# A decoder layer with 32 experts on one core: the two transposes of a unit side by side, two projection tiles in lockstep, and a table for the experts' order

## The chip, the cores and the metric
One core of one Trainium2 chip runs the whole layer in one launch, in float32. The metric is the device time in microseconds (us), median over runs.

## The reference
One inference step of a layer, for 1024 prompt tokens and 8 single-token samples, width 1024:
```python
u = layer_norm(x) * (1.0 + scale) + shift            # shift, scale, gates: m = silu(c) @ w_ada + b_ada
proj = u @ w_in                                      # 1024 -> 4624 columns
x_l, g_l, z, xbc, dt_raw = split(proj)
y_l = rms_norm(rglru(causal_conv(x_l)) * gelu(g_l))  # Griffin RG-LRU heads
y_s = rms_norm(ssd(silu(causal_conv(xbc)), dt) * silu(z))   # Mamba-2 heads
x = layer_norm(alpha * x + gate * (concat(y_l, y_s) @ w_out))
v = layer_norm(x) * (1.0 + scale2) + shift2
# top-1 group of 4, then top-2 of its 8 experts for each token
for each token t and each of its 2 experts e:
    f[t] += gate_weight * (silu(v[t] @ w_gate[e]) * (v[t] @ w_up[e])) @ w_down[e]     # 1024 -> 512 -> 1024
x = layer_norm(alpha * x + gate2 * f)
```
The counts of tokens by expert come out of the router at run time; any counts are allowed.

## The kernel before
Each engine has one program, and they meet by semaphores. The order of all work is written by hand; there is no scheduler. Products that need float32 accuracy are made from high and low halves (a slice of the left side times a slice of the right in the three combinations of PARTS).

**Front.** SP loads x tiles, pairs of columns of w_ada (`load_pair`) and the projection weights of a tile (`load_w`, 512 KB). VectorE normalises the eight tiles of x (L1132 to L1141), PE transposes each (`x_turn`, L885), GpSimd issues the small loads, b_ada in two layouts among them (badaP for the first two rows of modulation, bada4 for the others). Then the modulation: PE multiplies one of four pairs (`ada_pair`, L895), VectorE adds the bias (L1176), PE turns the result (L902), and VectorE scales two of the eight slices k of u by it and splits each into high and low (`u_pair`, `u_low` L1192). The projection of a tile of 128 columns (`project_split`, L939) is 72 matmuls: eight slices k, three PARTS, three pieces of 344 tokens. Its weights are split by ScalarE (`w_high`) and VectorE (`w_low`). Tile 0 goes slice by slice as u becomes ready, with pairs 2 and 3 of the modulation in it; tile 1 follows. Behind each of the first eight tiles stands a late pair (L877), which computes the remaining modulation rows. A tile's result is copied out before its PSUM bank is used again (`px_copied`).

**The experts.** 32 places in an order that the table rank_at gives: the first three places are experts 0 to 2, and the others get the remaining experts by rank of their number of units, rank 3 the largest; GpSimd writes the table with two iotas and copies, big ranks at every third place, small ones between. A unit is up to 32 tokens of one expert, a token being four rows of 256. For unit u:

- GpSimd gathers its rows of v into xg (L1851) by an index column that VectorE copies (icur, L2589), and stores its result by scur (L1859, L2593).
- PE turns the rows (`x_turn`, L2207), VectorE copies them to xT (`x_out`, L2577).
- PE multiplies with gate and up in four chunks q (`gate_up`, L2219, x64 in the trace, two records for each float32 matmul). ScalarE copies h out (`hb_out`, L1990) and makes its half of the activation (L1995).
- PE turns h (`h_turn`, L2228), VectorE forms the product (`h_out`, L2581, L2585), PE multiplies with down (`down`, L2237, x32), and ScalarE copies the result out (L2000).

PE's order is h_turn(u), gate_up(u+1), x_turn(u+2), down(u). VectorE's order is h_out(u), up_copy(u+2), gather_rows(u+4) and the rest. When unit u+2 starts a new expert, `up_copy` copies its up weights from the ring to wcur in four chunks (L2619), each after the matmuls that read that part of wcur, with x_out of the unit between the second and the third. ScalarE does the same with the gate weights (L2020), with hb_out between the second and the third. `down_copy` (L2632) moves the down weights behind the last down of the expert before.

SP loads all experts' weights into a ring with three slots for gate/up (4 MB) and two for down (2 MB). Its loop is serial, x from 2:
```python
sp.wait_ge(down_copied, copied_down(x - 1)); load_down(x + 1, e)
down_here(x)
gate_up_here(x + 1)
if 5 <= x + 2 < NE - 1:
    gate_up_when_copied(x + 2, x - 1)
if x + 3 == NE - 1:
    gate_up_when_copied(x + 3, x)
```
`gate_up_here` waits for the landing and tells ScalarE and VectorE; `gate_up_when_copied` waits until both have copied the weights that the slot held.

Of the kernel before, what the change touches and what calls it, by code (L numbers as in the profile page):

```python
# [25 lines left out]
ALU = mybir.AluOpType  # L26
# [54 lines left out]
def build_step(nc, x_prompt, x_sample, c_prompt, c_sample, state_lru_conv, state_lru_h, state_ssd_conv,  # L81
# [13 lines left out]
    with ctx:  # L95
# [113 lines left out]
        modP, badaP = at(46300, 4, P), at(43904, 4, P)  # L209
# [65 lines left out]
        bada_loaded = sem("bada_loaded")  # L275
        pair_loaded = [sem(f"pair_loaded{c}") for c in range(4)]
# [110 lines left out]
        with nc.Block() as block:  # L387
            @block.sync
            def _(sp):
# [113 lines left out]
            def _(gp):  # L503
# [8 lines left out]
                for g in range(4):  # L512
                    gp.dma_start(bada4[32 * g:32 * g + 32, :, :],
                                 b_ada.rearrange("a (r g n) -> g a r n", r=3, g=4)[g].to_broadcast([32, 3, 512]))\
                        .then_inc(bada_loaded, 16)
                for g in range(4):
                    gp.dma_start(badaP[32 * g:32 * g + 32, :, :],
                                 b_ada[:, 0:2 * D].rearrange("a (s c i n) -> s i a c n", s=2, c=4, i=2)[g // 2, g % 2]
                                 .to_broadcast([32, 4, P])).then_inc(bada_loaded, 16)
# [33 lines left out]
                gp.tensor_copy(qidx[:, :], itmp[:, :]).then_inc(gpsimd_once, 1)  # L553
                gp.wait_ge(xnT_mm, NT)
                for b in range(2):
                    gp.memset(xb2[b][:, 0:3], 0.0).then_inc(gpsimd_once, 1)

# [100 lines left out]
            def _(act):  # L658
# [57 lines left out]
                for k in range(KT):  # L716
                    if k == 5:
                        w_high(1, 0)
# [146 lines left out]
            def _(pe):  # L865
# [23 lines left out]
                def ada_pair(c):  # L889
                    pe.wait_ge(pair_loaded[c], 32)  # L890
                    if c > 1:
                        pe.wait_ge(mod0_ready, c - 1)
                    for k in range(KT):
# [27 lines left out]
                ada_pair(0)  # L921
                ada_pair(1)
# [3 lines left out]
                def project_split(b, w_round, by_slice=False, half_way=None):  # L926
                    pe.wait_ge(wh_ready[b], w_round + 1)
                    pe.wait_ge(wl_ready[b], w_round + 1)
                    for k in range(KT):
                        if half_way is not None and k == KT // 2:  # L930
                            half_way()
                        if by_slice and k in (2, 4):
                            ada_pair(k // 2 + 1)
# [1817 lines left out]
```

## Time and profile before
| what | value |
|---|---|
| median of 3 runs | 1520.05 us (1520.03 to 1522.19) |
| profiled execution | 1519.19 us |
| its span | 1517.4 us |
| mean granted clock of TensorE | 0.951 |
| PE busy | 1361.2 us, 90% |
| VectorE (DVE) busy | 969.7 us, 64% |
| ScalarE (ACT) busy | 574.1 us, 38% |
| GpSimd (POOL) busy | 296.7 us, 20% |
| mean DMA rate | 241 GB/s over the span |
| experts' stage | first gate_up at 913.29, last down ends at 1451.13 |

Times in a row are from the start of the span, and durations are in us. A row of a timeline gives in brackets how long the engine had been idle and what released it; "issue" means that it waited for nothing that the trace shows. PEld is the weight load, which overlaps PE. Matmul ends are modelled, so a run of matmuls in a row is read best from start to start.

### The profile page before, as it was taken

What the parts mean: (1) busy time and instruction counts of PE and PEld (TensorE: products, weight loads), DVE (VectorE), ACT (ScalarE), POOL (GpSimd) and SP (SyncE); (2) the same over time, 40 slices, a digit from 0 to 9 for tenths busy, and PEclk for the clock granted to TensorE, in tenths of its full rate; (3) what the DMA queues carried; (4) which work ended last, traced back from release to release, by engine and by line L of the source; (5) the groups of instructions that cost most, each with busy time, mean ns of one, the idle gap of its engine ahead of it and who ended that gap; (6) DMA issues with size and microseconds to landing.
All of it is one profiled execution on the core that took longest, in us unless ns stands there. A gap on an engine that the chain in (4) does not pass through costs nothing.

```text
span 1517.4 us, 38240 instructions
## 1 busy us (share of the span) xinstructions
PE 1361.2 (90%) x13487; PEld 1007.3 (66%) x13487; DVE 969.7 (64%) x1720; ACT 574.1 (38%) x886; POOL 296.7 (20%) x325
## 2 busy tenths in 40 slices
PE   4799999999999999799999539999999899999964
PEld 3688989899888889578588525554455455555421
DVE  6755553958999998888687674544454353351649
ACT  4322232535655555732132104433343243241532
POOL 4000002211000000200000013443333343443310
PEclk9899999999999999899999759999999999999987
DMA  9666414644333434932332948999999988979683
GB/s 279 220 228 247 144 42 157 210 154 143 114 113 114 123 117 155 337 105 70 99 90 81 367 187 321 416 409 415 413 409 398 404 356 367 400 283 416 265 322 153
DMA packets 145042, 365.87 MB, mean 241 GB/s; under 512 B 16072, under 2 KB 94976, under 8 KB 117192
## 3 DMA queue, kind: packets, MB, share of 16 engines
q1 hardware_dynamic: 126072, 308.72, 54.6%
q0 software_dynamic: 18320, 54.08, 10.0%
q10 hardware_dynamic: 576, 2.10, 0.4%
q8 instruction: 45, 0.74, 0.2%
q14 instruction: 29, 0.24, 0.0%
HBM read 324.06 MB, written 45.63 MB: 244 GB/s over the span
## 4 chain that ended last, share of the span: by engine, by line
PE 31%; DMA 16%; DVE 7%; issue 2%; SPq 1%; ACT 1%; ACTq 0%; DVEq 0%; POOLq 0%
DMA ring<-in_w_up_dram 14%; PE PS L2088 10%; PE PS L2219 10%; PE PS L2237 5%; DMA ring<-in_w_down_dram 2%; PE PS L2228 1%; DVE big L2289 1%; PE PS L2119 1%; PE PS L2207 1%; PE PS L2154 1%; DVE ring L2687 1%; DVE ring L2692 1%; PE PS L2111 1%; DVE ring L2701 1%; DVE big_end L2301 1%
## 5 line engine op out<-in xcount | busy, mean ns | idle before, releaser
L939 PE MATMUL PS<-big 128*128 128x344 f32 x2592 | 425.2, 324 | 1.7 <-DVE big L1192 1.7
L939 PEld LDWEIGHTS PS<-big 128*128 128x128 f32 x2592 | 414.2, 190 | 10.5 <-issue 6.7
L2219 PE MATMUL PS<-ring,arena 128*32 128x256 f32 x5248 | 306.4, 386 | 0.5 <-DVE arena L2577 0.5
L2219 PEld LDWEIGHTS PS<-ring,arena 128*32 128x32 f32 x5248 | 164.3, 111 | 113.5 <-issue 6.5
L2020 ACT ACTIVATE ring<-ring 128x1024 f32 x124 | 124.0, 1049 | 94.1 <-PE PS L2219 52.4
L2237 PE MATMUL PS<-ring,arena 128*32 128x256 f32 x2624 | 158.6, 382 | 1.0 <-DVE arena L2585 1.0
L1851 POOL DMA_INDIRECT arena<-v_d,icur x84 | 103.0, 1226 | 283.1 <-DVE icur L2589 191.3
L1859 POOL DMA_INDIRECT f_d<-arena,scur x82 | 107.7, 1313 | 55.3 <-issue 48.6
L2237 PEld LDWEIGHTS PS<-ring,arena 128*32 128x32 f32 x2624 | 77.0, 109 | 57.1 <-issue 13.4
L2581 DVE SCALAR_TENSOR_TENSOR arena<-arena,PS 128x128 f32<-128x128 f32 x82 | 23.6, 288 | 135.4 <-ACT arena L1995 97.5
L2577 DVE COPY arena<-PS 128x256 f32<-128x256 f32 x82 | 34.7, 423 | 103.9 <-PE PS L2207 103.8
L2619 DVE COPY ring<-ring 128x1024 f32 x124 | 80.6, 692 | 25.7 <-SPq L1712 20.0
L1990 ACT ACTIVATE arena<-PS 128x256 f32<-128x256 f32 x82 | 31.4, 382 | 170.2 <-PE PS L2219 170.2
L2088 PE MATMUL PS<-low 128*128 128x512 f32 x256 | 83.7, 409 | 10.5 <-issue 4.9
L2632 DVE COPY ring<-ring 128x4096 f32 x31 | 74.7, 2409 | 28.6 <-PE PS L2237 28.6
L2088 PE MATMUL PS<-big,low 128*128 128x512 f32 x256 | 81.3, 400 | 0.0
L2088 PE MATMUL PS<-low,big 128*128 128x512 f32 x256 | 81.0, 398 | 0.0
L2000 ACT ACTIVATE arena<-PS 128x256 f32<-128x256 f32 x82 | 31.4, 383 | 100.5 <-PE PS L2237 96.4
L2088 PEld LDWEIGHTS PS<-low 128*128 128x128 f32 x256 | 47.4, 194 | 21.7 <-issue 8.1
L1154 DVE TENSOR_TENSOR big<-arena,big 128x1024 fp32r<-128x1024 f32 x20 | 24.5, 1224 | 56.6 <-ACT big L713 56.5
L2228 PEld LDWEIGHTS PS<-ident,arena 128*128 128x128 f32 x164 | 26.0, 207 | 50.7 <-issue 29.6
L2228 PE MATMUL PS<-ident,arena 128*128 128x128 f32 x164 | 41.9, 338 | 16.9 <-ACT arena L1990 16.7
(473 smaller groups left out, 1876.5 us busy)
## 6 DMA issues: line engine op xcount, KB each, us to landing
ring<-in_w_gate_dram SPq DMA_DIRECT2D x32, 2048.0 KB, 9.6
ring<-in_w_up_dram SPq DMA_DIRECT2D x32, 2048.0 KB, 14.9
ring<-in_w_down_dram SPq DMA_DIRECT2D x32, 2048.0 KB, 8.1
arena<-in_w_ada_dram SPq DMA_DIRECT2D x16, 1024.0 KB, 6.7
arena<-in_w_in_dram SPq DMA_DIRECT2D x20, 512.0 KB, 7.8
upper<-in_w_ada_dram SPq DMA_DIRECT2D x8, 1024.0 KB, 11.6
upper<-in_w_in_dram SPq DMA_DIRECT2D x16, 512.0 KB, 4.0
arena<-acs_d SPq DMA_DIRECT2D x8, 1024.0 KB, 4.9
```

What stands on the lines that cost most here:

```text
L939: mm = pe.matmul(PS[:, 3 * b + a, 0:CU], wss[b][:, i, k, :], us[:, j, k, a * CU:(a + 1) * CU], start=(k == 0 and (i, j) == PARTS[0]), stop ...
L1851: gp.indirect_dma_start(xg[b], None, v_q, bass.IndirectOffsetOnAxis(ap=icur[b][:, :], axis=0), bounds_check=QW * (SEQ + DEC) - 1, oob_is_e ...
L1859: gp.indirect_dma_start(f_q, bass.IndirectOffsetOnAxis(ap=scur[b][:, :], axis=0), yo[b], None, bounds_check=QW * 2 * (SEQ + DEC) - 1, oob_ ...
L1990: act.activation(hb, PS[:, 3, 0:FH], ACT.Copy).then_inc(hb_ready, 1)
L2020: act.activation(wcur[:, 1024 * q:1024 * q + 1024], ring[:, bass.ds(w + 1024 * q, 1024)], ACT.Copy).then_inc(gate_copied, 1)
L2088: mm = pe.matmul(PS[:, bank + n, :], (yh[h % 2], yl3[h % 3])[a][:, k, :], (WH, WL)[b][i][:, 512 * n:512 * n + 512], start=(k == 0 and (a, ...
L2219: mm = pe.matmul(PS[32 * g:32 * g + 32, 3, 0:FH], xT[:, c, CAP * q:CAP * q + CAP], wcur[:, w:w + FH], start=(q == 0 and c == 0), stop=(q = ...
L2228: mm = pe.transpose(PS[:, 4, P * c:P * c + P], hb[:, c::2], ident[:, :])
L2237: mm = pe.matmul(PS[32 * g:32 * g + 32, 6, 0:DQ], hT[:, c % 2, CAP * (c // 2):CAP * (c // 2) + CAP], wcur[:, 8192 + 1024 * c + DQ * g:8192 ...
L2577: ve.tensor_copy(xT, PS[:, 0, 0:2 * P].rearrange("p (c t) -> p c t", c=2)).then_inc(xT_ready, 1)
L2619: ve.tensor_copy(wcur[:, 4096 + 1024 * q:5120 + 1024 * q], ring[:, bass.ds(w + (4096 + 1024 * q), 1024)]).then_inc(up_copied, 1)
L2632: ve.tensor_copy(wcur[:, GU:GU + DN], ring[:, bass.ds(w, DN)]).then_inc(down_copied, 1)
```

## The change
Three parts.

**Front.** SP posts the second tile's weights right behind the first's. The loads of badaP wait until PE has turned two tiles of x, those of bada4 until the last pair of w_ada has landed. The turn of a pair's modulation is a function of its own (`ss_turn`), and tiles 0 and 1 are computed slice by slice in turn: slice k of tile 0, then slice k of tile 1. VectorE makes the low half of the second tile's weights in front of slice 1 instead of slice 6, ScalarE its high half at k = 1 instead of 5. The late pairs stand one tile later, and the loop over the last four tiles is written out.

**Unit.** PE's order becomes h_turn(u), x_turn(u+2), gate_up(u+1), down(u); xT has two buffers; VectorE copies x and the index column at the start of its turn, ahead of h_out.

**Places.** The ranks come from a written table PLAN, one memset for each place from 3 on.

```diff
@@ SP
                 load_pair(0)
                 load_w(COL_XBC, 0)
+                load_w(COL_XBC + P, 1)
                 load_pair(1)
                 load_pair(2)
-                load_w(COL_XBC + P, 1)
                 load_pair(3)
@@ GpSimd, front (the two loops of loads stood ahead of the load of xt[NT])
+                gp.wait_ge(xnT_mm, 2)
+                for g in range(4):
+                    gp.dma_start(badaP[32 * g:32 * g + 32, :, :],
...
                 gp.wait_ge(xnT_mm, NT)
                 for b in range(2):
                     gp.memset(xb2[b][:, 0:3], 0.0).then_inc(gpsimd_once, 1)
+                gp.wait_ge(pair_loaded[3], 32)
+                for g in range(4):
+                    gp.dma_start(bada4[32 * g:32 * g + 32, :, :],
...
@@ ScalarE
                 for k in range(KT):
-                    if k == 5:
+                    if k == 1:
                         w_high(1, 0)
@@ PE, front
+                def ss_turn(c):
                     pe.wait_ge(mod0_ready, c + 1)
-                    if c > 1:
-                        pe.wait_ge(ss_ready, c - 1)
-                    pe.transpose(PS[:, 4 + c % 2, 0:P], modP[:, c, :], ident[:, :]).then_inc(ss_mm, 1)
+                    pe.transpose(PS[:, 6 + c % 2, P:2 * P], modP[:, c, :], ident[:, :]).then_inc(ss_mm, 1)
...
+                for k in range(KT):
+                    c = k // 2
+                    if k in (2, 4):
+                        ada_pair(c + 1)
+                    pe.wait_ge(uh_ready, k + 1)
+                    pe.wait_ge(ul_ready, k + 1)
+                    for b in range(2):
...
+                        mm = slice_products(b, k)
+                        if k == KT - 1:
+                            mm.then_inc(proj_mm[b], 1)
+                        if b == 0 and k % 2 == 0 and c < 3:
+                            ss_turn(c + 1)
...
+                late_pair(0)
+                for t in range(2, 12):
+                    pe.wait_ge(px_copied[t % 2], t // 2)
+                    project_split(t % 2, t // 2)
+                    if t < 9:
+                        late_pair(t - 1)
@@ VectorE, front
                 u_pair(0)
                 w_low(0, 0)
                 u_low(0)
+                u_pair(1)
+                w_low(1, 0)
                 u_low(1)
-                u_pair(1)
                 u_low(2)
                 u_low(3)
-                lam_rates()
                 u_pair(2)
                 u_low(4)
                 u_low(5)
                 u_pair(3)
-                w_low(1, 0)
...
+                lam_rates()
@@ experts, table
-        FIRST, EVERY = 3, 3
-        NBIG = (NE - FIRST) // EVERY
+        FIRST = 3
+        PLAN = [24, 23, 5, 16, 8, 7, 13, 3, 14, 26, 27, 6, 15, 4, 12, 28, 0, 11, 18, 22, 2, 19, 17, 9, 1, 25, 10, 20, 21]
...
+                step(gp.tensor_copy(rank_at[:, 0:FIRST], eidx[:, 0:FIRST]))
+                for x, r in enumerate(PLAN):
+                    step(gp.memset(rank_at[:, FIRST + x:FIRST + x + 1], float(FIRST + r)))
@@ experts, PE
                 with pe.Fori(1, pairs) as j:
                     for b in range(2):
                         h_turn(j * 2 + b)
-                        gate_up(j * 2 + (b + 1))
                         x_turn(j * 2 + (b + 2), j + 1, b)
+                        gate_up(j * 2 + (b + 1), 1 - b)
                         down(j * 2 + b)
@@ experts, VectorE
+                def x_out_next(u, b):
+                    ve.wait_ge(gu_mm, (u - 1) * QW)
+                    x_out(u, b)
...
                         for q in range(QW):
-                            if q == 2:
-                                x_out(u)
                             ve.wait_ge(gu_mm, before * QW + (q + 1))
...
                 with ve.Fori(1, pairs) as j:
                     for b in range(2):
+                        x_out_next(j * 2 + (b + 2), b)
+                        gather_rows(j * 2 + (b + 4), b)
                         h_out(j * 2 + b)
                         up_copy(j * 2 + (b + 2), j * 2 + (b + 1))
-                        gather_rows(j * 2 + (b + 4), b)
                         scatter_rows(j * 2 + b, j, b)
```

**The order on the engines.** First PE at the front, from the end of the transposes of x on. L895 (L899 after) is a pair of the modulation, L902 (L906) its turn, L939 (L934) the projection products, L877 (L880) a late pair. Before:
```order
L895 MATMUL PS<-upper 32x128 x32
L902 MATMUL PS<-ident,upper 128x128
L895 MATMUL PS<-upper 32x128 x32
L902 MATMUL PS<-ident,upper 128x128
L939 MATMUL PS<-big 128x344 x18
L895 MATMUL PS<-upper 32x128 x32
L902 MATMUL PS<-ident,upper 128x128
L939 MATMUL PS<-big 128x344 x18
```
and changed:
```order
L899 MATMUL PS<-upper 32x128 x32
L906 MATMUL PS<-ident,upper 128x128
L899 MATMUL PS<-upper 32x128 x32
L934 MATMUL PS<-big 128x344 x9
L906 MATMUL PS<-ident,upper 128x128
L934 MATMUL PS<-big 128x344 x27
L899 MATMUL PS<-upper 32x128 x32
L934 MATMUL PS<-big 128x344 x9
L906 MATMUL PS<-ident,upper 128x128
L934 MATMUL PS<-big 128x344 x27
```
Nine products now stand between a pair and its turn, and the products between two pairs are 36 instead of 18.

Second, PE in the experts' loop, one pair of units. L2228 (L2245) is the turn of h, L2219 (L2236) gate_up, L2207 (L2224) the turn of x, L2237 (L2254) down. Before:
```order
L2228 MATMUL PS<-ident,arena 128x128 x2
L2219 MATMUL PS<-ring,arena 32x256 x32
L2207 MATMUL PS<-ident,arena 128x128 x2
L2237 MATMUL PS<-ring,arena 32x256 x16
L2228 MATMUL PS<-ident,arena 128x128 x2
L2219 MATMUL PS<-ring,arena 32x256 x32
L2207 MATMUL PS<-ident,arena 128x128 x2
L2237 MATMUL PS<-ring,arena 32x256 x16
```
and changed:
```order
L2245 MATMUL PS<-ident,arena 128x128 x2
L2224 MATMUL PS<-ident,arena 128x128 x2
L2236 MATMUL PS<-ring,arena 32x256 x32
L2254 MATMUL PS<-ring,arena 32x256 x16
L2245 MATMUL PS<-ident,arena 128x128 x2
L2224 MATMUL PS<-ident,arena 128x128 x2
L2236 MATMUL PS<-ring,arena 32x256 x32
L2254 MATMUL PS<-ring,arena 32x256 x16
```
The turn of x moved from behind gate_up to ahead of it.

Third, VectorE in the experts' loop after the change, the head of a unit: L2593 copies x out, L2609 the index column of a gather, L2601 and L2605 form the product of h, L2637 copies up weights.
```order
L2593 COPY arena<-PS 128x256
L2609 COPY icur<-arena 128x1
L2601 SCALAR_TENSOR_TENSOR arena<-arena,PS 128x128
L2605 SCALAR_TENSOR_TENSOR arena<-arena,PS 128x128
L2631 COMPARE_AND_BRANCH
L2632 ISA
L2637 ISA
L2637 COPY ring<-ring 128x1024
```
Before, the copy of x (L2577) stood in the middle of the four weight copies (L2619), behind the product of h (L2581, L2585), and the index column after them.

## Rows read from the trace of the kernel before
**Rows 1.** Page, part 2: busy tenths of POOL and of the DMA engines, 40 slices
```profile
POOL 4000002211000000200000013443333343443310
...
DMA  9666414644333434932332948999999988979683
```

**Rows 2.** Chain of waits, 1318 to 1332: start us, us, what
```profile
1318.66 3.59 PE PS L2219 x64
1322.25 0.37 PE PS L2207 x2
1322.61 1.86 PE PS L2237 x32
1324.48 0.44 PE PS L2228 x2
```

**Rows 3.** Page, part 5: groups of the experts' gate_up and turn of h
```profile
L2219 PE MATMUL PS<-ring,arena 128*32 128x256 f32 x5248 | 306.4, 386 | 0.5 <-DVE arena L2577 0.5
...
L2228 PE MATMUL PS<-ident,arena 128*128 128x128 f32 x164 | 41.9, 338 | 16.9 <-ACT arena L1990 16.7
```

**Rows 4.** PE's timeline, 1415 to 1452: start us, us, engine, line [idle before <-releaser]
```profile
1433.99 0.50 PE L2228 MATMUL PS<-ident,arena 128*128 128x128 f32 x2 [3.09 <-ACT arena L1990]
1434.42 5.35 PE L2219 MATMUL PS<-ring,arena 128*32 128x256 f32 x64
...
1442.37 3.66 PE L2219 MATMUL PS<-ring,arena 128*32 128x256 f32 x64
1445.84 1.91 PE L2237 MATMUL PS<-ring,arena 128*32 128x256 f32 x32
```

**Rows 5.** VectorE's timeline at the front, 0 to 90
```profile
10.89 1.29 DVE L1132 BATCH_NORM_STATS2 lnst<-arena 128x6 f32<-128x512 f32 x2 [1.87 <-DMA arena<-in_x_prompt_dram]
...
16.10 1.29 DVE L1132 BATCH_NORM_STATS2 lnst<-arena 128x6 f32<-128x512 f32 x2 [0.94 <-DMA arena<-in_x_prompt_dram]
...
45.00 2.37 DVE L1192 TENSOR_TENSOR big<-arena,big 128x1032 fp32r<-128x1032 f32 x2
```

**Rows 6.** PE's timeline at the front, 0 to 100
```profile
27.82 1.09 PE L885 MATMUL PS<-ident,arena 128*128 128x128 f32 x8 [1.22 <-DVE arena L1141]
...
47.84 4.61 PE L939 MATMUL PS<-big 128*128 128x344 f32 x18
...
67.59 3.05 PE L939 MATMUL PS<-big 128*128 128x344 f32 x18 [1.70 <-DVE big L1192]
...
72.42 11.63 PE L939 MATMUL PS<-big 128*128 128x344 f32 x72
```

**Rows 7.** Timeline of all engines before place 18, 1176 to 1194
```profile
1184.92 0.70 PE L2228 MATMUL PS<-ident,arena 128*128 128x128 f32 x2 [6.41 <-ACT arena L1990]
...
1186.92 0.28 ACT L1995 ACTIVATE arena<-PS 128x128 f32<-128x128 f32 x1
...
1188.31 0.29 DVE L2585 SCALAR_TENSOR_TENSOR arena<-arena,PS 128x128 f32<-128x128 f32 x1
```

**Rows 8.** Timeline of all engines at the start of the experts' stage, 900 to 945
```profile
909.04 1.14 POOL L1851 DMA_INDIRECT arena<-v_d,icur  x1 [4.70 <-issue]
...
912.39 0.38 PE L2207 MATMUL PS<-ident,arena 128*128 128x128 f32 x2
...
914.14 1.00 POOL L1851 DMA_INDIRECT arena<-v_d,icur  x1 [2.63 <-DVE icur L2589]
...
921.48 0.20 PEld L2207 LDWEIGHTS PS<-ident,arena 128*128 128x128 f32 x2 [0.41 <-DMA arena<-v_d,icur]
```

**Rows 9.** The same timeline, last down of place 1; chain of waits, whole span (last three)
```profile
940.63 1.93 PE L2237 MATMUL PS<-ring,arena 128*32 128x256 f32 x32
...
948.24 16.53 DMA ring<-in_w_up_dram
966.73 14.71 DMA ring<-in_w_up_dram
...
1166.81 15.55 DMA ring<-in_w_up_dram
```

More of the change, by code:

```diff
@@ L511, in _ @@
                 gp.memset(cT, 0.0).then_inc(c_zeroed, 1)
[L512 to L519, printed above, removed]
                 gp.dma_start(xt[NT], x_sample[:, 0, :]).then_inc(xt_loaded[NT], 16)
@@ L921, in _, with slice_products, project_split @@
                 ada_pair(0)
+                ss_turn(0)
                 ada_pair(1)
                 PARTS = ((0, 0), (0, 1), (1, 0))
-                def project_split(b, w_round, by_slice=False, half_way=None):
+                def slice_products(b, k):
+                    for i, j in PARTS:
+                        for a in range(3):
+                            mm = pe.matmul(PS[:, 3 * b + a, 0:CU], wss[b][:, i, k, :], us[:, j, k, a * CU:(a + 1) * CU],
+                                           start=(k == 0 and (i, j) == PARTS[0]),
+                                           stop=(k == KT - 1 and (i, j) == PARTS[-1]))
+                    return mm
+                def project_split(b, w_round, half_way=None):
                     pe.wait_ge(wh_ready[b], w_round + 1)
@@ L952, in _ @@
                         ada(6 + n // KT, n % KT, late[n % 2]).then_inc(late_mm, 1)
-                with pe.Fori(4, 6) as i:
-                    for b in range(2):
-                        pe.wait_ge(px_copied[b], i)
-                        project_split(b, i)
+                late_pair(0)
[4 more added lines that the diff above has]
+                        late_pair(t - 1)
                 pe.wait_ge(uh_ready, KT + 1)
@@ L1165, in _ @@
                 ve.tensor_tensor(lamv[0], lamv[2], PT1[:, :, 7], ALU.max).then_inc(vector_once, 1)
[L1167 removed]
+                ve.wait_ge(bada_loaded, 64)
                 step(ve.tensor_scalar(badaP[64:128, :, :], badaP[64:128, :, :], 1.0, None, ALU.add))
[L1169 removed]
                 ve.wait_ge(xnT_ready, NT)
@@ L1244, in mod_out @@
                 def mod_out(r):
+                    if r == 1:
+                        ve.wait_ge(bada4_loaded, 64)
+                        step(ve.tensor_scalar(bada4[0:64, 2, :], bada4[0:64, 2, :], 1.0, None, ALU.add))
                     ve.wait_ge(late_mm, KT * r)
@@ L2208, in x_turn, with gate_up @@
                     mm.then_inc(eT_mm, 1)
-                def gate_up(u):
+                def gate_up(u, b):
                     pe.wait_ge(xT_ready, u + 1)
@@ L2244, in _ @@
                 x_turn(0, 0, 0)
-                gate_up(0)
+                gate_up(0, 0)
                 x_turn(1, 0, 1)
@@ L2248, in _ @@
                     h_turn(u)
-                    gate_up(u + 1)
                     x_turn(u + 2, 1, u)
+                    gate_up(u + 1, 1 - u)
                     down(u)
@@ L2254, in _ @@
                         h_turn(j * 2 + b)
-                        gate_up(j * 2 + (b + 1))
                         x_turn(j * 2 + (b + 2), j + 1, b)
+                        gate_up(j * 2 + (b + 1), 1 - b)
                         down(j * 2 + b)
                 h_turn(pairs * 2)
-                gate_up(pairs * 2 + 1)
+                gate_up(pairs * 2 + 1, 1)
                 down(pairs * 2)
```

61 lines of the change are left out of this document (24 added, 37 removed).

## The prediction
> **What bounds the kernel now.** I read the page first. PE (TensorE) is busy for 90% of the span, and the memory engines stand at nine tenths in nearly every slice from the twenty-fourth on, where the experts begin [rows 1]. So the experts' stage stands between two limits. The chain of waits says which one ends last: inside an expert it is PE alone, one unit in 6.26 us: gate_up 3.59, turn of x 0.37, down 1.86, turn of h 0.44 [rows 2]. Between some experts it is the load of the next gate/up weights. In the page's groups the turn of h (L2228) is the one with idle time before it, 16.7 us for ScalarE's L1990 [rows 3]; in PE's timeline these are four waits of 3.59, 3.65, 6.41 and 3.09, of which the last and the third stand in [rows 4, 7]. After each, gate_up runs at half clock: 5.35 after the last [rows 4], and over all 306.4 where 82 units of 3.66 are 300.1, so 6.3 for the four, 1.6 each [rows 3]. Two of the turns take 0.70 for 0.50. The four waits cost 16.7 + 6.3 + 0.4 = 23.4. By the counts of units they stand before places 9, 12, 18 and 31.
> Why a turn of h waits for a *load*: ScalarE copies h out (L1990) between the second and the third of the four chunks of the next expert's gate weights, so the last unit before a new expert cannot be turned until those weights have landed.
>
> **The front.** PE has two gaps to lose there. VectorE waits 1.87 and 0.94 for the first tiles of x [rows 5], while GpSimd's eight loads of b_ada run on the same memory engines; they now go later. Of 2.8 I take 2.3. Second, lockstep. Before, the first products start at 47.84 and tiles 0, 1 and the first late pair are done at 84.0 (72.42 and 11.63) [rows 6]. Now the first nine products start as before at u_low(0)'s end, 46.2 (45.00 and half of 2.37) [rows 5]; behind them the turn, two scalings and w_low(1,0) let the second tile begin at about 52.4. From there 135 products at 0.1615 (11.63/72) are 21.8, two pairs of ada 3.9, two turns 0.6, together 78.7; 0.8 for products at half clock (4.61/18 is 0.256 each at the start) and 1.86 for the late pair give 81.3: 2.7 less. VectorE covers it: its last slice was ready at 67.59 [rows 6], while PE now asks for it at about 76. From 5.0 I keep back 0.5 for ScalarE's second weight copy, which now stands ahead of slice 1. **Front: -4.5**, between 0 (x waits for its own bytes, lockstep only swaps waits) and -6.5. At no cost: lam_rates and the scaling of bada4, on VectorE behind the last slice, where it waits for PE's tiles; the unrolled tiles; 29 memsets of the table on GpSimd, which is idle for most of the middle [rows 1]. If that cover were gone, the memsets would cost some 4 us.
>
> **The unit.** Before, each turn pair stands alone. Now the turn of x follows the turn of h, and down follows gate_up. The last gate_up of the stage already runs straight into its down: 1442.37 to 1445.84, 3.47 instead of 3.59 [rows 4]; likewise (3.66 - 1.93)/32 is 54.1 ns a record, 64 of them 3.46. So 0.13 goes. Eight transposes in a row take 1.09 [rows 6], a pair 0.44 [rows 8]: (1.09 - 0.44)/6 = 0.108 for each further one, 0.22 for a second pair instead of 0.37: 0.15. Of 0.28 I take 0.25; bounds 0.13 (only the first half) and 0.28. New period 6.01; over 79 units **-19.8**. What covers the rest: down needs VectorE's product of h, which ended 2.98 after the turn of h in a unit (1188.60 against 1185.62) [rows 7]; now 0.22 and 3.46 lie between, 3.68. VectorE's copy of x and two short index copies, some 0.7 together, now stand ahead of that product, but it waits anyway for ScalarE's L1995, which ends 1.6 after the turn (1187.20) [rows 7].
>
> **The start of the stage.** The turn of x(2) moves ahead of gate_up(1), from 921.48 to about 917.9. Its gather was issued at 914.14; the weight load at 921.48 is the only one of L2207 in the stage that was released by a gather, where the others show issue, with the same 0.41 of idle time [rows 8]. So it had landed just before 921.1, or within the 0.41. PE then waits 3.1, and half clock costs 1.5 more: **+4.6**, between 0 and +5. Against it the Trainium skill ("DMA: Bandwidth & Descriptors", Queues, rings and completion order) says that each DMA engine takes packets from its queues in turn, so that a small gather would not stand behind the large loads issued by SP. By that rule the term would be 0. The row at 921.48 speaks against it and does not settle it.
>
> **The places.** The new table gives the experts by units as 1,3,1,1,1,4,2,3,3,2,6,2,1,1,3,2,5,2,1,9,2,1,1,7,1,1,2,8,1,2,1,2 (before: 1,3,1,3,2,2,3,2,2,3,2,2,4,2,2,5,1,1,6,1,1,7,1,1,8,1,1,9,1,1,1,2). Both are the same 82 units (5248 records of 64 a unit) [rows 3]. At each place I compare three times for the turn that needs its weights, in the time frame of before.
> (a) PE's own time, 6.01 a unit.
> (b) The loads' queue. SP posts down of place p-1 only when down of p-3 is copied, that is after the last down of p-4 has ended (at T), and gate/up of p behind it. For place 5 the trace of before has the whole way: T = 940.63 + 1.93 = 942.56, up issued at 948.24 and landed at 964.77 [rows 9]; from a landing to the turn it is 2.56 (1166.81 + 15.55 = 1182.36, turn at 1184.92) [rows 7, 9]. So T + 24.8. With four units in places p-3 to p-1, PE wants the turn at T + 18.0; with three, at T + 12.0.
> (c) The bus. Where loads follow without a pause, one place's come every 16.67 (966.73 to 1166.81 in 12) [rows 9].
> Place 5 (three units before it): 24.8 - 12.0 = 12.8, and 1.6 for the clock: 14.4. Place 14 (four): 6.8 + 1.6 = 8.4; by (c) alone 4.2. Places 16 and 19 come by (c), two and three loads later: 1.7 and 1.9. Places 23 and 27 (four): 8.4 each. Place 31: its load goes out when the gate/up of 28 has been copied. Before, with three units (18.8) ahead, the wait was 3.1, so it needs 21.9; now four (24.0) are ahead: nothing. No other place has fewer than five units before it, and none of them is reached by (c). Sum 14.4 + 3 x 8.4 + 3.6 = 43.2, against 23.4 now: **+19.8**; bounds +13 (place 14 by (c), half of the waits at 23 and 27 gone because the bus is idle ahead of them) and +23.
>
> **The sum.** -4.5 - 19.8 + 4.6 + 19.8 = +0.1. The profiled execution took 1519.19, 0.86 under the median of 1520.05; I forecast 1519.3 for one like it and **1520.2** as the median. About 0.2% (3.0 us) is what a measurement of this kernel can tell from no change; this is within it.
>
> **The rivals.**
> A, *the gather is there*: the start costs nothing, and the front gives up to 6.5. For it: the first gather, issued at 909.04, was used at 912.39, 2.2 after its issue had ended; the same would bring this one at 917.4, in time [rows 8]. Against: the loads of 4 MB that start at the same moment, and the releaser at 921.48. 1520.2 - 4.6 = 1515.6, down to 1513.6.
> B, *only half of the stretch is saved*, the slower side: a second pair of transposes behind the first costs 0.37 as before, because it waits for its own operands. For it: the two pairs read and write other buffers than one another, unlike the eight in a row. Against: those eight at 0.108. The saving is then 0.13. The 37 units between places 5 and 19 go by the loads anyway, so 0.12 is lost on some 42 units, 5.0: 1525.2. It decides from a saving below 0.18 (2.9/42 under 0.25).
> C, *the loads are later than computed*: in the busy stretch they share the bus with gathers and stores that come sooner now; or the weights of projection tile t+3, posted only one tile ahead, are late. 1 us at each of five places is +5: 1525.2.
> D, *the table costs less*: at 14, 23 and 27 the bus has been idle, and the loads land sooner. -6: 1514.2.
> E, *lockstep does nothing*, since VectorE sets the pace of both tiles: +2.2, 1522.4. Against it: 67.59 above.
>
> **How the numbers follow.** Forecast 0.46 (1516.5 to 1523.9; 0.08 faster, 0.32 same, 0.06 slower). A 0.19 faster. B 0.14 (0.02 same, 0.12 slower). C 0.10 (0.03 same, 0.07 slower). D 0.07 faster. E 0.04 same. Faster 0.34, same 0.41, slower 0.25. The range, 1512.5 to 1527, reaches past A and D below and past B and C above; outside lie two of these together.
>
> **What would show it.** In the chain of waits a unit of 6.01: gate_up to down 3.46, two turns together in 0.66; a unit of 6.13 would be B. PE waits before the turns of places 5 (12.8), 14, 23 and 27 (6.8 each), 16 and 19 (under 2), none before 31. A PE wait of 3.1 before the turn of x(2) at the stage's start; without it, A. Tiles 0 and 1 and the first late pair done at about 79 (81.3 less the 2.3). The forecast is wrong in its working, even if the time fits, where the saving of a unit or the sum of those waits is off by more than a third.

## The result and the profile after
The changed kernel took 1547.26 us (median of 5, 1542.91 to 1554.02) against 1521.41 for the kernel before beside it: a ratio of 1.0171, 95% interval 1.0156 to 1.0186, so 26 us slower. The forecast was 1520.2 with a range to 1527. The profiled execution is the slowest of the five (1554.02), and its sums are made against its own span.

The page of the changed kernel, to be held against [rows 1, 3]; the last line is gate_up, by its new line:
```profile
span 1552.4 us, 38135 instructions
...
PEclk8899999999999999899999589999999999999977
DMA  9566516543433445732225938999699957979684
...
L2236 PE MATMUL PS<-ring,arena 128*32 128x256 f32 x5248 | 325.6, 386 | 4.7 <-issue 2.2
```
The experts' slices show the memory engines less full than before in three places (6, 5 and 7 tenths where 9, 8 and 8 stood), and gate_up is busy for 325.6 instead of 306.4, though the waits that halve its clock are again four. The stage took 562.9 from the first turn of h to the last (919.23 to 1482.10) instead of 530.2 (917.45 to 1447.69): 32.6 more of the 35.0 by which the spans differ; the rest is 1.8 in front of the stage and 0.6 behind it.

**The front.** VectorE's timeline has one wait for x left, PE's timeline the lockstep:
```profile
10.07 1.29 DVE L1152 BATCH_NORM_STATS2 lnst<-arena 128x6 f32<-128x512 f32 x2 [1.29 <-DMA arena<-in_x_prompt_dram]
```
```profile
45.79 1.74 PE L934 MATMUL PS<-big 128*128 128x344 f32 x9 [2.59 <-ACT big L724]
...
51.13 5.80 PE L934 MATMUL PS<-big 128*128 128x344 f32 x27 [3.38 <-DVE big L1174]
...
68.18 10.18 PE L934 MATMUL PS<-big 128*128 128x344 f32 x63
78.30 1.92 PE L880 MATMUL PS<-arena,upper 128*32 128x512 f32 x16
80.15 11.62 PE L934 MATMUL PS<-big 128*128 128x344 f32 x72
```
1.29 is waited instead of 1.87 and 0.94. Tiles 0 and 1 and the first late pair are done at 80.15 instead of 84.0: 3.9. But this lead is gone before the experts begin: their stage starts 1.8 later than before, so 5.7 are lost between. Two pieces of it can be named, and neither belongs to the change: PE's work from 340.65 to 393.61 takes 1.6 more than before, which after_third (the same kernel again, below) does not show, and a wait of 2.02 for VectorE at 657, which plan_only has with the old front. Executions differ in this part: the first turn of h stands between 914.6 and 921.0 in the six traces with the old front and between 911.2 (front_only) and 919.2 (this one) in the thirteen with the new.

**An ordinary unit** (all engines' timeline, place 11; L1868 is the gather):
```profile
1109.58 0.51 PE L2245 MATMUL PS<-ident,arena 128*128 128x128 f32 x2
...
1109.93 0.38 PE L2224 MATMUL PS<-ident,arena 128*128 128x128 f32 x2
...
1110.24 3.66 PE L2236 MATMUL PS<-ring,arena 128*32 128x256 f32 x64
...
1113.72 1.91 PE L2254 MATMUL PS<-ring,arena 128*32 128x256 f32 x32
...
1113.96 1.43 POOL L1868 DMA_INDIRECT arena<-v_d,icur  x1 [0.89 <-DVE icur L2609]
...
1115.56 0.51 PE L2245 MATMUL PS<-ident,arena 128*128 128x128 f32 x2
```
The turn of x follows 0.35 after the turn of h, gate_up 0.31 later, down 3.48 after gate_up; the next unit begins 5.98 after this one (5.97 in most units), 0.29 under 6.26. The gather stands here behind gate_up, because VectorE was copying an expert's weights.

**The start, and the waits for weights** (PE's timeline at three places):
```profile
919.23 0.50 PE L2245 MATMUL PS<-ident,arena 128*128 128x128 f32 x2
922.88 0.41 PE L2224 MATMUL PS<-ident,arena 128*128 128x128 f32 x2 [3.15 <-DMA arena<-v_d,icur]
923.22 3.66 PE L2236 MATMUL PS<-ring,arena 128*32 128x256 f32 x64
```
```profile
972.25 0.70 PE L2245 MATMUL PS<-ident,arena 128*128 128x128 f32 x2 [11.83 <-ACT arena L2007]
```
```profile
1134.58 0.70 PE L2245 MATMUL PS<-ident,arena 128*128 128x128 f32 x2 [7.00 <-ACT arena L2007]
```
The turn of x(2) waits 3.15 for its gather, as forecast; PE waits 11.83 before place 5 and 7.00 before place 14, and 6.40 and 6.12 before places 23 and 27. All turns of h together:
```profile
L2245 PE MATMUL PS<-ident,arena 128*128 128x128 f32 x164 | 42.3, 340 | 31.5 <-ACT arena L2007 31.4
```
31.4 for ScalarE's L2007, against 16.7.

**A unit inside an expert** (place 10), the same view; L1876 is the store, PEld the weight load:
```profile
1082.56 0.51 PE L2245 MATMUL PS<-ident,arena 128*128 128x128 f32 x2
...
1083.21 4.23 PE L2236 MATMUL PS<-ring,arena 128*32 128x256 f32 x61
...
1084.25 1.03 POOL L1876 DMA_INDIRECT f_d<-arena,scur  x1 [4.41 <-DVE icur L2609]
...
1085.59 1.02 POOL L1868 DMA_INDIRECT arena<-v_d,icur  x1 [0.31 <-issue]
1086.24 0.16 PEld L2236 LDWEIGHTS PS<-ring,arena 128*32 128x32 f32 x3 [0.28 <-issue]
1086.99 0.19 PEld L2236 LDWEIGHTS PS<-ring,arena 128*32 128x32 f32 x5 [0.59 <-issue]
...
1087.11 1.80 PEld L2254 LDWEIGHTS PS<-ring,arena 128*32 128x32 f32 x32
...
1089.32 0.50 PE L2245 MATMUL PS<-ident,arena 128*128 128x128 f32 x2
```
This was not forecast. There are no copies here, VectorE is early, and GpSimd issues the gather (1085.59) right behind the store (1084.25), in the middle of gate_up. 2.75 into gate_up the stream of weight loads stops, for 0.28 and again for 0.59, with the releaser "issue": PE waited for nothing that the profile shows. The unit takes 6.76 instead of 5.97. I call this a break. 39 units of this trace take 6.4 to 7.3, 31.9 more than 39 of 5.97. The stop goes with the gather: that starts 2.8 to 3.6 after the turn of h in the units with a break, the weight loads stop some 0.4 behind it and, for the longer time, 0.8 to 1.0 behind it. The units with the gather between 3.7 and 4.2 all take 5.97. The stop goes with the issue of the gather and not with its data: in 19 of the 41 units with the gather at 2.8 to 3.6, no packet of GpSimd's queue is on the way in the 1.5 after the gather's start, and they too take 6.4 or more.

The stage adds up: -0.29 x 81 = -23.5 for the units; +3.3 at the start; 41.1 at the four places against 23.2, +17.9; and 34.9 for the 39 breaks (31.9) and ten units with some 0.3 each, most of them ahead of a new expert. Together 32.6.

### The profile page after: what moved, and what is told of

It is laid out like the page before. It is cut to its first block, busy times and chain, and to the rows that moved or that the text cites. A ratio compares the mean times of both kernels' runs of the same rounds, so it can differ in the third digit from the quotient of the medians.

```text
span 1552.4 us, 38135 instructions
## 1 busy us (share of the span) xinstructions
PE 1373.0 (88%) x13487; PEld 1041.7 (67%) x13487; DVE 968.5 (62%) x1720; ACT 574.3 (37%) x886; POOL 283.0 (18%) x350
## 4 chain that ended last, share of the span: by engine, by line
PE 42%; DVE 7%; DMA 5%; issue 2%; DVEq 1%; ACT 1%; SPq 1%; ACTq 0%; POOLq 0%
PE PS L2236 16%; PE PS L2105 10%; PE PS L2254 9%; DMA ring<-in_w_up_dram 4%; PE PS L2245 2%; DVE big L2306 1%; PE PS L2224 1%; PE PS L2136 1%; PE PS L2171 1%; DVE ring L2707 1%; DVE ring L2649 1%; DVE ring L2712 1%; PE PS L2128 1%; DVE ring L2721 1%; DVE big_end L2318 0%
## 5 line engine op out<-in xcount | busy, mean ns | idle before, releaser
L934 PE MATMUL PS<-big 128*128 128x344 f32 x2592 | 428.5, 326 | 6.0 <-DVE big L1174 3.4
L934 PEld LDWEIGHTS PS<-big 128*128 128x128 f32 x2592 | 417.2, 192 | 15.5 <-issue 10.9
L2236 PE MATMUL PS<-ring,arena 128*32 128x256 f32 x5248 | 325.6, 386 | 4.7 <-issue 2.2
L2236 PEld LDWEIGHTS PS<-ring,arena 128*32 128x32 f32 x5248 | 167.7, 111 | 136.9 <-issue 41.1
L2254 PE MATMUL PS<-ring,arena 128*32 128x256 f32 x2624 | 174.4, 380 | 3.3 <-DVE arena L2605 1.0
L1876 POOL DMA_INDIRECT f_d<-arena,scur x82 | 102.3, 1248 | 327.8 <-ACT arena L2017 261.2
L2593 DVE COPY arena<-PS 128x256 f32<-128x256 f32 x82 | 34.8, 425 | 191.5 <-PE PS L2224 143.5
L2254 PEld LDWEIGHTS PS<-ring,arena 128*32 128x32 f32 x2624 | 107.6, 110 | 50.8 <-DVE arena L2605 11.0
L2637 DVE COPY ring<-ring 128x1024 f32 x124 | 81.5, 709 | 52.4 <-SPq L1734 30.1
L2649 DVE COPY ring<-ring 128x4096 f32 x31 | 71.0, 2290 | 61.7 <-PE PS L2254 61.7
L2007 ACT ACTIVATE arena<-PS 128x256 f32<-128x256 f32 x82 | 31.3, 381 | 199.5 <-PE PS L2236 199.5
L1868 POOL DMA_INDIRECT arena<-v_d,icur x84 | 93.8, 1117 | 57.9 <-DVE icur L2609 30.9
L2245 PE MATMUL PS<-ident,arena 128*128 128x128 f32 x164 | 42.3, 340 | 31.5 <-ACT arena L2007 31.4
L2245 PEld LDWEIGHTS PS<-ident,arena 128*128 128x128 f32 x164 | 25.9, 207 | 65.3 <-ACT arena L2007 34.1
L2017 ACT ACTIVATE arena<-PS 128x256 f32<-128x256 f32 x82 | 31.4, 383 | 87.7 <-PE PS L2254 84.2
L2105 PEld LDWEIGHTS PS<-low,big 128*128 128x128 f32 x256 | 49.4, 193 | 11.0
L2105 PEld LDWEIGHTS PS<-big,low 128*128 128x128 f32 x256 | 49.4, 193 | 10.9
## 6 DMA issues: line engine op xcount, KB each, us to landing
upper<-in_w_ada_dram SPq DMA_DIRECT2D x8, 1024.0 KB, 11.9
```

The costliest lines, as they stand in the source:

```text
L934: mm = pe.matmul(PS[:, 3 * b + a, 0:CU], wss[b][:, i, k, :], us[:, j, k, a * CU:(a + 1) * CU], start=(k == 0 and (i, j) == PARTS[0]), stop ...
L1868: gp.indirect_dma_start(xg[b], None, v_q, bass.IndirectOffsetOnAxis(ap=icur[b][:, :], axis=0), bounds_check=QW * (SEQ + DEC) - 1, oob_is_e ...
L1876: gp.indirect_dma_start(f_q, bass.IndirectOffsetOnAxis(ap=scur[b][:, :], axis=0), yo[b], None, bounds_check=QW * 2 * (SEQ + DEC) - 1, oob_ ...
L2017: act.activation(yo[b], PS[:, 6, 0:DQ], ACT.Copy).then_inc(yo_ready, 1)
L2105: mm = pe.matmul(PS[:, bank + n, :], (yh[h % 2], yl3[h % 3])[a][:, k, :], (WH, WL)[b][i][:, 512 * n:512 * n + 512], start=(k == 0 and (a, ...
L2236: mm = pe.matmul(PS[32 * g:32 * g + 32, 3, 0:FH], xT[b][:, c, CAP * q:CAP * q + CAP], wcur[:, w:w + FH], start=(q == 0 and c == 0), stop=( ...
```

## The experiments
Ratios are to the kernel before, run in the same group.

### First group: the parts, and a later gather
`gather_late`:
```diff
-                def gather(u, b):
+                def gather(u, b, done=None):
                     gp.wait_ge(icur_ready, u + 1)
+                    if done is not None:
+                        gp.wait_ge(gu_mm, done * QW)
...
+                        gather(j * 2 + (b + 4), b, j * 2 + (b + 2))
```
So the gather of unit u+4 waits until PE has finished gate_up(u+1).

> The changed kernel, with one more wait on GpSimd: the gather of unit u+4 is issued only when gate_up(u+1) has ended. Theory G (in the changed kernel PE's stream breaks off for 0.5 to 0.8 us in some 37 units because the gather is issued right behind a scatter in the middle of gate_up): the breaks go, units of 6.7 to 6.9 become 5.97, and the time falls by up to 37 x 0.8 = 28, less what the weights' loads take back: 1519 to 1527. Rival S (the breaks come from PE having no pause of its own between gate_up and down any more, whatever GpSimd does): they stay, 1545 to 1550.

`turns_only`, `plan_only`, `front_only`: the kernel before with the hunks of one part of the change.

> The kernel before with the new order of a unit alone (old table, old front). Theory G and rival S: breaks in the units that bring no new expert's weights, about as many as in the changed kernel, 1524 to 1535. Rival T (the breaks need the new table): none, units of 5.97 all through, 0.29 less on 79 units, 4.7 more at the start and some 8 given back at the loads: about 1511.

> The kernel before with the new table of ranks alone. Units stay at 6.26 without breaks under every theory but T. The waits by the prediction's rules with 6.26 a unit: place 5 12.3 + 1.6, places 14, 23 and 27 6.0 + 1.6 each, places 16 and 19 about 1 together, 38 in all against 23.4: 14 to 15 slower, 1535 to 1536. If loads land sooner on an idle bus (rival D of the prediction) 1529.

> The kernel before with the new front alone. In the changed kernel tiles 0 and 1 and the first late pair were done at 80.15 against 84.0 before, so 3.8 faster if nothing behind it gives it back: 1517 to 1518. If later waits (weights of a projection tile) take it back: 1521.

| kernel | median | ratio (95%) |
|---|---|---|
| before | 1517.08 | |
| gather_late | 1522.04 | 1.0035 (1.0017 to 1.0052) |
| turns_only | 1515.12 | 0.9985 (0.9969 to 1.0002) |
| plan_only | 1531.74 | 1.0102 (1.0080 to 1.0123) |
| front_only | 1512.16 | 0.9980 (0.9963 to 0.9996) |

The table alone costs 1.0%. Its units are 6.26, and its waits are those of the rule; the first one in PE's timeline (L2223 is the turn of h):
```profile
966.67 0.70 PE L2223 MATMUL PS<-ident,arena 128*128 128x128 f32 x2 [11.80 <-ACT arena L1985]
```
11.80 before place 5 (12.3 expected), 5.95, 5.96 and 6.01 before 14, 23 and 27 (6.0 each). The front brings 0.2%. turns_only has no breaks, although its gathers stand close behind a store, 3.0 after the turn of h, as in the changed kernel: taken alone, rival T is right, although the time is 1515 and not the 1511 that was expected. gather_late has none either, which would fit G. What this group could not tell is whether the changed kernel itself would have had any in it.

### Second group: what do the breaks need?
`front_turns` and `turns_plan` are two of the three parts each; `after_again` is the changed kernel; `after_pad` moves its loop in the program:
```diff
+                pad = pe.alloc_register("pad")
+                for n in range(40):
+                    pe.reg_mov(pad, n)
                 x_turn(0, 0, 0)
```


> The changed kernel itself, beside the others of this group. If the breaks in PE's stream belong to the kernel, it is 1.5 to 1.9% over the kernel before, with some 35 units of 6.7 to 6.9. If they belonged to the chip on which it was first run, the units are 5.97 and it comes out as gather_late did, 0.2 to 0.5% over.

> The new front and the new order of a unit, with the old table. Theory A (the breaks need the place in PE's program at which the new front puts the loop, together with a gather close behind a scatter): breaks in the units without new weights, 0.8 each, 1 to 1.5% over the kernel before. Rival T (the breaks need the new table): none, and the two parts add: 0.35% under it, about 5.3 us.

> The new order of a unit and the new table, with the old front. Theory A: no breaks, turns_only and plan_only add, 0.8 to 1% over the kernel before. Rival T: breaks, 2% over or more.

> The changed kernel with 40 register moves in PE's program ahead of the experts' part, which only shift the loop to another place in the program. Theory A: other units break, or none, the time changes by many times the cost of 40 register moves (at most 2 us). Theory G or the table alone: about as many breaks as in the changed kernel.

| kernel | median | ratio (95%) | units of 6.4 to 7.3, their excess |
|---|---|---|---|
| before | 1520.60 | | |
| after_again | 1553.69 | 1.0215 (1.0184 to 1.0246) | 41, 36.0 |
| front_turns | 1530.58 | 1.0070 (1.0048 to 1.0091) | 43, 36.4 |
| turns_plan | 1557.57 | 1.0241 (1.0214 to 1.0268) | 41, 35.5 |
| after_pad | 1552.79 | 1.0206 (1.0163 to 1.0249) | 41, 36.0 |

All four have them, with either table and either front, so T and A both fall, and the place of the loop in the program does not matter. (Six of the 43 long units of front_turns have the gather after 4.0 and are longer for other reasons; 37, with 31.7 in excess, are like the one shown.) But turns_only, whose loop is that of turns_plan, had none. Either it differs in some other way, or the group does.

### Third group: the kernel or the group?
`after_third`, `turns_only_2` and `gather_late_2` are kernels of above; `best_try` is front_turns with the later gather and, for unit 0, the old order:
```diff
                     h_turn(u)
+                    if u == 0:
+                        gate_up(1, 1)
                     x_turn(u + 2, 1, u)
-                    gate_up(u + 1, 1 - u)
+                    if u == 1:
+                        gate_up(2, 0)
                     down(u)
```
VectorE's copies for unit 0 stand in the old order as well.

> The changed kernel once more, as the control for the other three of this group. If the breaks in PE's stream come and go with the group of runs and not with the kernel, it is now either 2% over the kernel before (breaks) or 0.3% over it (none), and the others follow it.

> The new order of a unit alone, a second time: the first time it had no breaks, while front_turns and turns_plan, with the same loop, had them in a later group. Theory K (kernel): none again, 0.1 to 0.2% under the kernel before. Theory R (the group of runs, such as where the program and its buffers lie): breaks like those of after_third in this group, 0.8% over.

> The gather issued only behind gate_up(u+1), a second time, now beside the changed kernel itself. Theory G (a gather close behind a scatter in the middle of gate_up causes the breaks): none here even where after_third has them, 0.3 to 0.5% over the kernel before against 1.7 to 2.2%. If the first run was free of breaks only because its whole group was: as slow as after_third.

> New front, new order of a unit, old table, the gather late as in gather_late, and for the first unit alone the old order (gate_up before the turn of x). If the parts add and there are no breaks: 1% under gather_late for the table, 5 us more for the start: about 0.9% under the kernel before, 1507. With breaks as in front_turns less the start: 0.4% over.

| kernel | median | ratio (95%) |
|---|---|---|
| before | 1515.93 | |
| after_third | 1519.11 | 1.0028 (1.0014 to 1.0042) |
| turns_only_2 | 1513.46 | 0.9980 (0.9963 to 0.9997) |
| gather_late_2 | 1520.40 | 1.0021 (1.0007 to 1.0035) |
| best_try | 1505.85 | 0.9941 (0.9920 to 0.9962) |

The changed kernel, unaltered, is now 0.3% over the kernel before, where it had been 1.7 and 2.2%. The same code, in a unit of the same place 10 as the one with a break, with the store at 2.16 and the gather at 3.51 after the turn (all engines' timeline of after_third):
```profile
1086.01 0.51 PE L2245 MATMUL PS<-ident,arena 128*128 128x128 f32 x2
...
1086.66 3.66 PE L2236 MATMUL PS<-ring,arena 128*32 128x256 f32 x64
...
1088.17 1.02 POOL L1876 DMA_INDIRECT f_d<-arena,scur  x1 [3.70 <-ACT arena L2017]
...
1089.52 1.02 POOL L1868 DMA_INDIRECT arena<-v_d,icur  x1 [0.32 <-issue]
...
1090.14 1.91 PE L2254 MATMUL PS<-ring,arena 128*32 128x256 f32 x32
...
1091.98 0.39 PE L2245 MATMUL PS<-ident,arena 128*128 128x128 f32 x1
```
gate_up 3.66, unit 5.97, and no unit of the trace lies between 6.4 and 7.3. So the breaks come and go with the group of runs (theory R), and my reading of turns_only in the first group was wrong. The chip alone does not decide it: the record gives the first group, without breaks, and the second, with them, the same chip number. The kernel before is not untouched either: its median is 1521.4, 1520.6 and 1520.2 in the three groups with breaks (the first measurement, the second and the fourth group) and 1517.1, 1515.9 and 1515.6 in the three without. Its only trace has units of 6.26, and no trace of it was kept from a later group, so where it loses these 3 to 6 us is not known.

best_try is 0.6% under the kernel before, where 0.9% had been expected, and 13.3 us under the changed kernel in the same group, mostly by its table. Its own order for unit 0 brought little: units 0, 1 and 3 are now 0.9, 1.7 and 1.2 too long, 3.8, where unit 0 alone is 3.0 to 5.9 too long in the traces with the new order. gather_late_2 (1.0021) and after_third (1.0028) do not differ, so the later gather costs nothing that can be measured where there are no breaks.

### Fourth group: does the later gather take them away?


> Control of this group: front and turns with the old table and the gather not delayed. In a group of runs with breaks in PE's stream 0.7% over the kernel before, with some 50 longer units; in one without them 0.35% under it.

> The same with the gather issued only behind gate_up(u+1) and the old order for the first unit. If the control has breaks: theory G says none here, units of 5.97 and about 0.6% under the kernel before as in the third group; rival S says breaks here too, 0.2 to 0.4% over it. If the control has none, it says only what the third group said, 0.6% under.

This group had breaks: front_turns_2 1.0058 (1.0037 to 1.0079), 40 units of 6.4 to 7.3 with 31.9 in excess (37 of them with the gather at 2.8 to 3.6, 29.5); best_try_2 **0.9956** (0.9933 to 0.9979), 1514.13 against 1520.24. A unit inside place 21 in each, first front_turns_2 (L2241 gate_up, L1881 store, L1873 gather), then best_try_2 (L2243, L1883, L1875):
```profile
1261.28 0.51 PE L2250 MATMUL PS<-ident,arena 128*128 128x128 f32 x2
...
1261.94 4.23 PE L2241 MATMUL PS<-ring,arena 128*32 128x256 f32 x61
...
1262.94 1.03 POOL L1881 DMA_INDIRECT f_d<-arena,scur  x1 [4.05 <-ACT arena L2022]
...
1264.27 1.03 POOL L1873 DMA_INDIRECT arena<-v_d,icur  x1 [0.30 <-issue]
```
```profile
1252.32 0.51 PE L2252 MATMUL PS<-ident,arena 128*128 128x128 f32 x2
...
1252.97 3.66 PE L2243 MATMUL PS<-ring,arena 128*32 128x256 f32 x64
...
1254.60 1.03 POOL L1883 DMA_INDIRECT f_d<-arena,scur  x1 [2.03 <-issue]
...
1256.45 1.91 PE L2261 MATMUL PS<-ring,arena 128*32 128x256 f32 x32
...
1257.54 1.02 POOL L1875 DMA_INDIRECT arena<-v_d,icur  x1 [1.91 <-PE PS L2243]
...
1258.29 0.51 PE L2252 MATMUL PS<-ident,arena 128*128 128x128 f32 x2
```
With the gather behind gate_up (at 5.2) gate_up is 3.66 again and the unit 5.97, in nearly every unit that brings no new expert. Theory G holds there for PE's stream, S falls. Not all is gone: best_try_2 still has 16 units of 6.4 to 7.3, 11.8 in excess, where best_try has two, 2.1. In them nothing stops in gate_up; in 15 of them PE waits for VectorE's product before down, 11.9 in the whole stage against 1.2 in best_try (1.0 of it, before the last down, in both). The same unit 47 in the timeline of all engines (L2659 copies the down weights), best_try first, then best_try_2 with its gather (L1875) and with PE's down (L2261) waiting for the product:
```profile
1226.52 2.29 DVE L2659 COPY ring<-ring 128x4096 f32 x1 [0.35 <-PE PS L2261]
```
```profile
1226.68 1.17 POOL L1875 DMA_INDIRECT arena<-v_d,icur  x1 [2.41 <-issue]
...
1228.18 2.29 DVE L2659 COPY ring<-ring 128x4096 f32 x1 [1.16 <-PE PS L2261]
...
1231.98 1.93 PE L2261 MATMUL PS<-ring,arena 128*32 128x256 f32 x32 [0.61 <-DVE arena L2615]
```
The copy begins 0.31 after the turn of h in best_try and 1.12 after it in best_try_2. This is no single case: best_try begins all 25 such copies 0.30 to 0.32 after the turn, best_try_2 21 of them 0.56 to 1.95 after it, most at 0.8, and then 1.5 to 1.7 behind the start of a gather, as here (1226.68 to 1228.18). In the unit with a break above, PE's second stop ends 1.40 behind the gather's start. So in this group with breaks VectorE is late where its copy falls into that time behind a gather. Most of these gathers stand some 3 behind a store: for VectorE a store close ahead is not needed.

### Fifth group: which order of gather and store?
`gather_first` is front_turns with gather(k+5) ahead of scatter(k) on GpSimd. `before_swap` is the kernel before with scatter(k), the store, ahead of gather(k+4); its edit:
```diff
                     for b in range(2):
-                        gather(j * 2 + (b + 4), b)
                         scatter(j * 2 + b, b)
+                        gather(j * 2 + (b + 4), b)
```


> Control of this group: 0.6 to 0.7% over the kernel before if the group has breaks in PE's stream, 0.35% under it if not.

> front_turns with GpSimd's order turned round: the gather of unit k+5 is issued ahead of the store of unit k, so at about 2.0 after the turn of h instead of 3.0, and the store behind it. If the control has breaks: theory G1 (a gather close behind a store is what breaks PE's stream) says none here, 0.3% under the kernel before; theory G2 (either of two indirect transfers in the middle of gate_up) says as many as in the control, only at another place.

> The kernel before with GpSimd's order turned round the other way: the store of unit k, and right behind it the gather of unit k+4, in the middle of gate_up, with PE's old order. If the control has breaks: theory G1 says breaks here too, some 40 x 0.7, 1.5% over the kernel before; theory P (the breaks need a PE that goes from gate_up into down without its own short pause) says none, no difference from the kernel before.

The control had no breaks: front_turns_3 0.9955 (0.9941 to 0.9968), gather_first 1.0043 (1.0024 to 1.0061), before_swap 1.0021 (1.0006 to 1.0036). So the group tells nothing on G1, G2 and P. It shows only that either order has waits of its own: 27 units of gather_first are 0.15 to 1.5 too long, 14.3 in all, most of it PE's wait for VectorE, and in before_swap PE waits 5.3 in all for gathers.

The traces of the groups with breaks do say something on G1 and G2, because the gathers in them do not all stand at one distance from the store. Six of these traces have the early gather (after, after_again, after_pad, front_turns, turns_plan, front_turns_2). The distance is from the store's start to the gather's:

| gather after the turn of h | behind the store | six traces with breaks | four without (after_third, front_turns_3, both turns_only) |
|---|---|---|---|
| 3.2 | 1.54 to 1.56 | 13 units of 6.4 to 6.5, one of 6.8 | 11 units of 5.97 |
| 3.7 to 4.2 | 1.6 or more | 46 gathers, no stop | 24, no stop |
| 3.8 to 4.4 | 1.33 | 26 gathers, 13 with a stop of 0.44 to 0.60 | 25, no stop |

The last two rows have the gather at about the same time of the unit, and only the one close behind a store is followed by a stop (for instance in front_turns at 4.08, in a unit of 7.02). This speaks for G1 and against G2 as far as PE goes. It is read from units that happened to lie so, and not from a kernel that was changed in this alone.

## Why the prediction was wrong
- **The unit** is the step that failed. "New period 6.01; over 79 units -19.8" named as cover only VectorE and ScalarE. The 5.97 is right where nothing breaks, and the units then bring -23.5; but in the first measurement 39 units took 0.8 more, +31.9 in the trace, and ten more some 0.3, so that the units came to +11.4 where -19.8 had been put. The later gather takes the stops of PE away in front_turns's place (fourth group). I moved the gather's issue into the middle of gate_up without pricing it: the text counted its index copy on VectorE, 0.15, and not what GpSimd does next. No rival had it: B, the slower side, was the turns, which are 0.04 better than forecast; C named sooner gathers, but as load on the bus, and the breaks come without such load (below).
- **The places**: +19.8 forecast, +17.9 measured. Place 5 waited 11.83 for 12.8 and place 14 7.00 for 6.8; 23 and 27 6.40 and 6.12 for 6.8. The small waits by the bus did not come at 16 and 19 where the breaks slowed PE; in after_third one of 1.9 stands before place 18. plan_only, 14.7 over the kernel before, is the 14 to 15 that the rules give at 6.26.
- **The start**: 3.15 waited for 3.1, half clock in some traces only (gate_up 3.66 in the first, 5.35 in after_third, where the granted clock is 0.68 of full speed over it). +3.3 for 4.6. Rival A was wrong: the gather was late, with the large loads just begun. The Trainium skill ("DMA: Bandwidth & Descriptors", Queues, rings and completion order) states that the queues take turns packet by packet. The trace agrees so far: the gather's 48 packets move from 919.96 to 922.33 with 109 packets of the loads among them, while the 48 of the gather before it, alone, took from 914.01 to 914.84. But they begin 4.05 after the gather's start instead of 1.73, and so the term was not 0, as the prediction read the rule.
- **The front**: 3.9 in the trace for 4.5 forecast, but of this nothing was left at the experts: +1.8 in front of the stage, 6.3 off the forecast, which the trace does not put down to the change. front_only is 0.2% faster (interval 0.04 to 0.37%).
- **The sum** of the stage was +4.6 in the forecast. In the third group it was 533.6 (911.76 to 1445.36) for 530.2 in the only trace of the kernel before, +3.4, and the whole kernel 1.0028 of the kernel before, inside the range. So without breaks the table's cost and the unit's gain nearly cancel, as forecast. The stage of the changed kernel was 29.3 longer in the first measurement than in the third group, and the breaks of the first are 31.9. The forecast holds in one of the three groups in which the changed kernel ran; it said nothing of what sets them apart.

**What stays open.** What differs between groups of runs, and why the issue of a gather then stops PE. It is not the load on the memory engines. Two units of the changed kernel (us, busy time of PE, PEld, DVE, ACT, POOL, clock, DMA share, GB/s):
```profile
core 0: us, PE busy (x) PEld busy (x) DVE busy (x) ACT busy (x) POOL busy (x), PEclk, DMA share, GB/s
...
1102.71:1109.58 6.87, 6.73 (x101) 3.95 (x100) 1.12 (x5) 2.02 (x5) 2.05 (x2) 1.00 0.10 32
1109.58:1115.56 5.98, 5.98 (x101) 3.42 (x101) 5.03 (x8) 4.15 (x7) 3.19 (x2) 1.00 0.35 90
```
The first, at 32 GB/s, has a break of 0.9; the second, with more traffic but the gather behind gate_up, has none. Nor is it the clock, 1.00 in both. VectorE is late behind a gather as well (L2659 above), which suggests something that the engines share, such as the supply of instructions or the passing on of semaphores; this is argued and not shown. Whether a gather ahead of the store would leave PE alone, and whether the kernel before would break with the gather close behind the store (P), was not settled, since the fifth group had no breaks.

## What to carry to other kernels
An instruction that is moved on one engine moves what it releases on another: here the copy of an index column moved a gather from between two units into the middle of a long run of matmuls. Price the transfer at its new place. And run the changed kernel itself as a control in several groups of runs: one and the same program was 0.3% over the kernel before in one group and 2.2% in another, and a variant that is measured once, in a group without breaks, looks cured. And where a load needs 25 us, three experts in a row with three or four units of 6 us in all cost 6 to 12 us each time. The version to keep is best_try: the new front and the new order of a unit, the old table, and the gather behind gate_up. It is 0.6% (third group, without breaks) and 0.4% (fourth, with them) under the kernel before.

## What the runs showed of the hardware that I had not expected
PE's stream of weight loads can stop for 0.6 with nothing to wait for that the profile shows, 0.8 to 1.0 after GpSimd begins an indirect gather 1.33 behind a store, in about half of the cases while no packet of GpSimd's queue moves. In the first measurement and the second and fourth group this met every unit with the gather 2.8 to 3.6 after the turn of h (38 to 41 of an execution), and none of 46 gathers at 3.7 to 4.2 that stood 1.6 or more behind the store; in the first, third and fifth group, with the same program or the same loop, the traces with the same early gather have no such stop. In the fourth group VectorE was late behind gathers at 5.2. The kernel before has 6.26 in all ordinary units of its one trace; but there the gathers stand 0.2 to 0.4 before the turn of h or 0.9 to 1.6 after it (one at 2.45), so it never had one at the place that matters.
